# Two token sets through the second transformer block, as one program in lockstep or as two interleaved ones

## What is computed

```
for i in range(2):
    m, mc = 9 modulation vectors each, from silu(c) @ w_ada[i] and silu(c_ctx) @ w_ada[i]
    h  = h  + 0.5 * m[2]  * swiglu(modulate(rms_norm(h)),  w13_ffn1[i], w2_ffn1[i])
    hc = hc + 0.5 * mc[2] * swiglu(modulate(rms_norm(hc)), w13_ffn1[i], w2_ffn1[i])
    z  = modulate(rms_norm(h),  m[3],  m[4])  @ w_in[i]
    zc = modulate(rms_norm(hc), mc[3], mc[4]) @ w_in[i]      # layer 1: key and value columns alone
    keys and values k, v from z; kc, vc from zc
    y  = [fourier, attention over (k, kc), spatial gating, pooling](z) @ w_out[i]
    h  = h + m[5] * y
    h  = h + 0.5 * m[8] * swiglu(modulate(rms_norm(h)), w13_ffn2[i], w2_ffn2[i])
    if i == 0:
        yc = the same four mixers of zc, attention over kc alone, @ w_out[i]
        hc = hc + mc[5] * yc
        hc = hc + 0.5 * mc[8] * swiglu(modulate(rms_norm(hc)), w13_ffn2[i], w2_ffn2[i])
return rms_norm(h)
```

## Time and profile before

| | us |
|---|---|
| median of 3 runs | 4091.4 (4089.8 to 4098.1) |
| the profiled execution, its own time | 4091.2 |
| its span, first to last instruction | 4089.2 |
| TensorE busy | 3689.9 (90%) |
| VectorE busy | 2266.3 (55%) |
| ScalarE busy | 1085.0 (27%) |

### The profile page before, as it was taken

One profiled execution on the slowest core, in us unless ns is written; L12 is line 12 of the kernel. 1 busy time (PEld: TensorE's weight loads), 2 busy tenths in 40 slices (PEclk: granted clock), 3 DMA queues, 4 the chain that ended last, 5 costly groups with the idle time before them and its releaser, 6 DMA issues. The chain is left out here.

```text
span 4089.2 us, 47364 instructions
## 1 busy us (share of the span) xinstructions
PE 3689.9 (90%) x19008; PEld 2975.7 (73%) x19008; DVE 2266.3 (55%) x5134; ACT 1085.0 (27%) x1685; POOL 331.2 (8%) x293
## 2 busy tenths in 40 slices
PE   5898998999889999877889999998999997788998
PEld 3655886788678888755547888887888884457886
DVE  5564556655666666744345666676666434434334
ACT  3354002322331111233243212123212133233222
POOL 1012001100120000111101000012000011001000
PEclk9998887999989999988999999998999997898998
DMA  5532003344323333333102333332343312112332
GB/s 158 149 93 74 1 1 88 108 121 121 93 62 98 106 101 104 89 95 94 46 16 79 94 106 93 111 96 78 93 113 94 92 48 83 30 42 80 96 93 67
DMA packets 663803, 348.33 MB, mean 85 GB/s; under 512 B 29989, under 2 KB 658919, under 8 KB 663328
## 3 DMA queue, kind: packets, MB, share of 16 engines
q1 hardware_dynamic: 662432, 342.69, 29.8%
q10 hardware_dynamic: 1152, 2.62, 0.2%
HBM read 340.55 MB, written 4.72 MB: 84 GB/s over the span
## 5 line engine op out<-in xcount | busy, mean ns | idle before, releaser
L1748 PE MATMUL psum<-hn_high,high 128*128 128x512 f32 (+2 forms) x3360 | 1235.8, 368 | 149.3 <-DVE hn_low L2153 59.6
L1750 PE MATMUL psum<-hn_high,low 128*128 128x512 f32 (+2 forms) x3360 | 1207.6, 359 | 0.0
L1749 PE MATMUL psum<-hn_low,high 128*128 128x512 f32 (+2 forms) x3360 | 1207.3, 359 | 0.0
L1748 PEld LDWEIGHTS psum<-hn_high,high 128*128 128x128 f32 (+1 forms) x3360 | 642.0, 191 | 283.7 <-DVE hn_low L2153 64.4
L1750 PEld LDWEIGHTS psum<-hn_high,low 128*128 128x128 f32 (+1 forms) x3360 | 640.8, 191 | 104.0 <-issue 2.3
L1749 PEld LDWEIGHTS psum<-hn_low,high 128*128 128x128 f32 (+1 forms) x3360 | 643.0, 191 | 95.2 <-issue 3.4
L2123 DVE TENSOR_TENSOR low<-stage,high 128x1024 fp32r<-128x1024 f32 (+3 forms) x440 | 527.8, 1219 | 209.0 <-ACT high L1450 208.2
L2178 DVE SCALAR_TENSOR_TENSOR partial<-stage,cond,partial 128x128 f32<-128x128 f32 x2304 | 626.4, 348 | 0.0
L1450 ACT ACTIVATE high<-stage 128x1024 fp32r<-128x1024 f32 (+3 forms) x440 | 436.9, 1016 | 502.5 <-DMA stage<-in_w_ffn 362.7
L1748 PE MATMUL psum<-hidden_high,high 128*128 128x512 f32 (+1 forms) x1408 | 500.7, 356 | 5.0 <-DVE low L2123 5.0
L1750 PE MATMUL psum<-hidden_high,low 128*128 128x512 f32 (+1 forms) x1408 | 492.5, 350 | 0.0
(11 more groups left out here) (307 smaller groups left out, 3258.6 us busy)
## 6 DMA issues: line engine op xcount, KB each, us to landing
stage<-in_w_ffn SPq DMA_DIRECT2D x240, 512.0 KB, 4.5
stage<-in_w_ada SPq DMA_DIRECT2D x192, 512.0 KB, 3.9
stage<-in_w_in SPq DMA_DIRECT2D x56, 512.0 KB, 5.1
stage<-in_w_out SPq DMA_DIRECT2D x32, 512.0 KB, 4.2
stage<-in_w_ffn SPq DMA_DIRECT2D x32, 384.0 KB, 3.8
stage<-in_w_gate SPq DMA_DIRECT2D x22, 512.0 KB, 3.9
stage<-in_w_up SPq DMA_DIRECT2D x22, 512.0 KB, 5.2
stage<-in_w_down SPq DMA_DIRECT2D x16, 512.0 KB, 4.2
```

The lines of the kernel that those rows point to most:

```text
L1748: self.e.matmul(out, high[:, i], xh, start=first and i == 0, stop=False)
L1749: self.e.matmul(out, high[:, i], xl, start=False, stop=False)
L1750: done = self.e.matmul(out, low[:, i], xh, start=False, stop=last and i == nk - 1)
```

## The change

The walk's steps of the second block become generators, and two of them are run against each other: `lead_stream`, the main tokens', and `side_stream`, the context's. Each `yield` hands back an expected time to wait before the stream has something ready. `together` keeps a clock of its own, to which `cost` adds an estimate for products, and takes among the streams that are due the one that comes out of a wait first, else the one that is preferred: the context's until its first mixers are done (`urgent`), then the main tokens'. The order so found is fixed when the program is built.

Each stream asks for its own weight blocks, so that those of three half steps are loaded and split for the context once more. The context goes by groups of 4 and 3 tiles (`GROUPS_SIDE`; its down blocks are 256 columns wide in groups of 4), the main tokens in the first half step by groups of 6 and 5 (`GROUPS_BESIDE`), since both sets' tiles must now lie in memory together. Main products can be parted after four of eight tiles. The main tokens have two PSUM banks and the context two, and the context has four temporaries of its own. A context tile asks for a modulation job at every second tile; main tiles at each, and at two of eight down blocks. The Fourier tables come as blocks through the stages instead of one large transfer. The main attention has two pairs of banks for scores, and its transposes go by three into single banks. The norm between the blocks is part of the main tokens' stream, and so lies beside the context's first half step. The first half step's norm of the context was in the first block already.

```
+GROUPS_BESIDE = ((0, 6), (6, 6), (12, 5), (17, 5))
+GROUPS_SIDE = ((0, 4), (4, 4), (8, 4), (12, 4), (16, 3), (19, 3))
...
+    def together(self, lead, side):
+
+        ready, waited = {lead: self.now, side: self.now}, {lead: False, side: False}
+        while ready:
+            streams = [x for x in ((side, lead) if self.side.urgent else (lead, side)) if x in ready]
+            due = sorted((x for x in streams if ready[x] <= self.now), key=lambda x: not waited[x])
+            stream = due[0] if due else min(streams, key=ready.get)
+            self.now = max(self.now, ready[stream])
+            gap = next(stream, None)
+            if gap is None:
+                del ready[stream]
+            else:
+                ready[stream], waited[stream] = self.now + gap, gap > 0
...
-    def swiglu(self, name, parts, w_a, a0, w_b, b0, w_down, gate, meanwhile=None):
-        for first, tiles in GROUPS:
+    def swiglu(self, name, part, groups, hidden, w_a, a0, w_b, b0, w_down, gate, meanwhile=None):
+        halves = ((0, KT // 2), (KT // 2, KT)) if part is self.main else ((0, KT),)
+        for first, tiles in groups:
...
+                n, slot, view = self.weights(w_b, 0, KT, b0 + at * P)
+                if at and (part is self.main or at % 2):
                     self.pump_background()
...
+            yield max(0.0, 3.0 - 0.7 * (tiles - 1))
...
+                if self.events and part is self.main and f % 4 == 1:
                     self.pump_background()
...
     def second_block(self):
-        main, side = self.main, self.side
-        for layer in range(2):
...
-            self.norm_for_half_step(main, layer, "g_ffn1", 0)
-            self.half_step([main, side], layer, "g_ffn1", 0)
-            self.mixers(side, layer, layer == 1)
-            self.mixers(main, layer, False)
...
+        main.banks, side.banks = Turn(self.banks.spots[0:2]), Turn(self.banks.spots[2:4])
+        self.events.add("second")
+        self.together(self.lead_stream(), self.side_stream())
...
+    def lead_stream(self):
+        yield from self.plain_norm(main, "final", True)
+        for layer in range(2):
+            yield from self.half_step(main, layer, "g_ffn1", 0, ...)
+            while layer == 0 and "side mixed" not in self.events:
+                yield 3.0
+            yield from self.mixers(main, layer, False)
...
+            yield from self.half_step(main, layer, "g_ffn2", 6, GROUPS, hidden["whole"])
...
+    def side_stream(self):
+        side.urgent = True
+        yield from self.half_step(side, 0, "g_ffn1", 0, GROUPS_SIDE, hidden, normed=True)
+        yield from self.mixers(side, 0, False)
+        side.urgent = False
+        self.events |= {"side mixed", ("kv", 0)}
...
+        yield from self.half_step(side, 0, "g_ffn2", 6, GROUPS_SIDE, hidden)
+        yield from self.half_step(side, 1, "g_ffn1", 0, GROUPS_SIDE, hidden)
+        while ("attention", (0, "main")) not in self.events:
+            yield 3.0
+        yield from self.mixers(side, 1, True)
+        self.events.add(("kv", 1))
```

705 lines of the change are left out of this document (407 added, 298 removed).

## The result

The changed kernel takes 4358.5 us (median, 4357.4 to 4360.4), the kernel before 4090.8 beside it; the ratio is 1.0656 (95% interval 1.0643 to 1.0670). The forecast was 4108 with a range to 4190: the direction was right, the size was not. The loss is 268 us instead of 17.

The account below looks back on a forecast made before the run. TensorE, 90% busy, was taken as the bound, leaving only its idle and half-clock time to win. Losses of 184 us less gains of 167 made it 17 us slower: 4108 us, own range 4075 to 4150, full range 4025 to 4190.

Parts of the forecast that it names:

- Item b: Context tiles alone: TensorE waits 0.37 us per tile, 2.7 with a job; 46 us slower, plus 17 for later stretches.
- item a: Job bursts before the context's first mixers and second half step: TensorE stands 88 us; with clock, 100 us slower.
- item c: Twelve modulation jobs between main down products, each making TensorE wait 0.9 to 2.7 us: 21 us slower.
- gains 1 to 5: Savings by stage from interleaved work, from the norm between the blocks through layer 1: 167 us faster together.
- Gains 1 and 2: Other work beneath the norm between the blocks (27 us) and beneath half steps' entry norms and group ends (48 us).
- Gains 3 to 5: Less loss in the context's mixers (29 us), main mixers of layer 0 (35 us) and layer 1 (28 us).
- gain 4: Main mixers of layer 0: context blocks after score rows and in most other gaps win 50 of 85, less clock and queue: 35 us faster.
- The attention rival: Layer 0's main attention: VectorE and ScalarE queue, steps take 8 to 9 us instead of 6.8; total 4178 us, chance 0.24.
- The rival's other half: 25 jobs inside both mixers cost 1.6 us more each, 40 us slower; chance 0.24 for the whole rival.
- The window gap: Main mixers: gaps of 3 to 7 us behind the window operations would still be there.
- Its clock, 12 us: Lower granted clock after the two bursts of jobs adds 6 us for each burst.
- the three signs named for a wrong forecast: Bursts shorter than 60 us, context tiles at 5.7 us, or layer 0 attention steps over 8 us would refute the forecast.

Follow-up runs that it names:

- few sums: 14 of 16 VectorE operations of each second-block modulation job left out: changed kernel 4150.9 us, kernel before 4057.4 us; also called short sums.
- the parted kernel: Kernel before, each half step parted into main tokens' then context's with own weight blocks, nothing interleaved: 4290.2 us; 4179.9 with short sums.
- the doubled: Kernel before, order kept, weight blocks in half steps of both token sets loaded and split again for the context: 4315.1 us; 4190.3 with short sums.

## Why the prediction was wrong, step by step

Item b of the prediction is parted here into its jobs (37) and the rest (26), item a is 100 and item c 21:

| term | forecast | measured |
|---|---|---|
| jobs in bursts (item a) | 100 slower | 92 slower (56 by their sums, 36 left with few sums) |
| jobs in context tiles and between down blocks (b in part, c) | 58 slower | 121 slower (151 - 30) |
| all else: own blocks 26 slower (rest of b), gains 1 to 5 167 faster | 141 faster | 58 slower (94 - 36) |
| sum | 17 slower | 271 slower |

The measured column adds up by construction, because its rows are differences of kernels, good to some 10 us. The first row came near. The step that failed is in the third: 199 of the 254 us by which the forecast is short. The prediction let a filler cover a gap as if its weights and its bank were ready, and charged it 26 us of waits of its own; with few sums the new waits for low halves and banks are 124 us, and only 87 us of the old ones went away. The second row failed by 63 us.

By stages, us lost (length less busy time x clock), with few sums and without the bursts:

| stage | before | forecast without jobs | measured |
|---|---|---|---|
| norm between the blocks, the context's first half step | 27 | 16 | 59 |
| the context's mixers | 54 | 25 | 33 |
| main half steps, with what lies beside them | 72 | 33 | 77 |
| main mixers of layer 0 | 85 | 50 | 72 |
| layer 1, mixers to output | 96 | 68 | 132 |

- **What bounds the kernel, and the busy times**: right. VectorE at 58% is no bound on average. The prediction then wrote that everything hangs on where it is waited for, and costed only the places where it is busy. In the ring above VectorE is idle for 1.65 us of each 4.57.
- **Gains 1 and 2** (75) did not come. The step was "beneath the norm the order now has 12 context blocks, 34 us of work over a loss of 27: gain 27". It took the filler's products from the order and forgot the filler's split, which stands in ScalarE's and VectorE's queues between the norm's steps. The 19.0 us wait of the earlier trace rows is gone, and the stage loses 59 us where 16 were forecast. The first stage lasted 343 us where some 300 were forecast; 27 of the 343 are a burst. Taking the fillers out again cost nothing and saved up to 20 us. What those at the group ends brought was not measured apart.
- **Gains 3 to 5** (92) came in part. The context's mixers gained 21 of 29 us. In the main mixers of layer 0 the nine waits for scores (11.6 us) are gone, but new waits, those for banks above all (18 us with few sums), leave 13 of the 35 us of gain 4. In layer 1 nothing was won: 132 us lost where 68 were forecast and 96 were lost before, and jobs aren't the reason, since with whole jobs it is 129. A part of it is that 186 us of context work now lie in these stages, with its own waits. The Trainium skill, Perfetto Trace Analysis, Optimization Strategy, says that interleaving regimes in which different engines are the most contended may improve performance. In this case's traces it took away the waits for scores, and not the loss in the norms, where both streams need the same queues in turn; the whole was 6.6% slower.
- **The attention rival** (steps of 8 to 9 us): where a context down block stands between, score rows of layer 0 follow each other every 5.1 us (2353.44 to 2358.52). Over 15 rows (2347.46 to 2449.93) a step takes 7.3 us, between the 6.8 of the forecast and the rival. Two waits of 5.1 us for a job's addition are in it, where the prediction said that none would be over 3. The rival's other half came: jobs in and around the mixers. With short sums the fourth stage is 52 us shorter, some 6 of it a burst of two, where the rival had 40. The window gap stood as forecast (7.46 us at 2185.15).
- **Item a** (bursts): 92 us of standing, forecast 88. **Its clock, 12 us**, was the only clock among the losses; items b and c had none. TensorE's busy time rose by 74 us in all, for the same products. The granted clock of the whole stretch fell from 0.95 to 0.93.
- **Item b** was too small, 63 with its later stretches, though its single tiles were priced nearly right: in the parted kernel a bare context tile repeats every 6.34 us, with a wait of 0.42 in it (forecast 6.0 with 0.37). In the changed kernel two context tiles, one with a job, take 16.35 us (VectorE's first multiplications at 1302.48 and 1318.83), forecast 14.8. The wait behind the job is 2.60 us, forecast 2.7, but not for the low half: both low halves were made before the job, and TensorE waits for a bank until the multiplication behind the job:

```profile
1302.94 0.45 PE L1910 MATMUL psum<-hn_high,high 128*128 128x256 f32 x1 [2.60 <-DVE side_tmp L2571]
```

  So the price was right by luck, for another wait. And the 0.37 was taken for the context alone. Behind a main tile the chain is 3.6 us instead of 3.2, in the norm's ring a round is 4.6, and there are many more such places than the tiles that I counted: 236 blocks more, each with its own chance to be late.
- **Item c** (12 jobs between down blocks, 21 us): of the right kind and too short a list. Jobs outside bursts cost 121 us more than before where some 58 were forecast. A job is nearly free under a tile of both token sets (121 jobs cost 30 us) and dear where a block of 2.83 us is what covers it.
- None of the three signs named for a wrong forecast showed (bursts under 60 us, tiles at 5.7 us, attention steps over 8 us on the mean). They tested the terms that were in the sum, and the missing ones were not in it.

Open is how the 124 us of new waits in the changed kernel split into what its own blocks cost and what the two banks of each stream cost: the doubled and the parted kernel have their own orders and four banks, and no kernel with two streams and more banks was built.

## What to carry to other kernels

Before work is put into another engine's gap, write down everything that it needs on the other engines, and where that stands in their queues: a filler whose operand is made by the engine that is late is itself late. A block shared by two users costs one preparation over the sum of their products; parted, the smaller user has the same preparation under a third of the products. Look, too, at who frees the output's bank: with few banks, that step's place in its queue counts as much as the operand's. If the gaps are there because the next operand stands behind a chain, preparing one more operand ahead is the small change to try first: here it brought 1.2%, and the rebuilt order cost 6.6%.

## What was not expected of the hardware

GpSimd took 1.91 us for a multiplication of 128 x 1024 numbers, and a multiplication of VectorE that ran beside it (1442.04) took 0.68 us, as one alone did before. Jobs in a row come no faster than one in 1.8 us, even when the sums are nearly empty; VectorE then waits for the transfers. A table load took 1283 ns in all 64 places of the changed kernel. The Trainium skill (ScalarE: Activation LUTs, What ACT_TABLE_LOAD costs) gives the same for the load and adds a drain of about 1380 ns, 2.66 us together. This case's trace agrees on the load and shows no such drain: 38 of the 64 have the next operation within 0.1 us, and ScalarE was idle for 0.4 us in all before the 23 of this line:

```profile
L1801 ACT ACT_TABLE_LOAD x23 | 29.5, 1283 | 0.4
```
